# Decay sums of a state space branch: the mask stationary, the masked decays moving in two rounded parts, two step tiles for four

## What is computed

```python
def segsum_exp(a):                       # a: log decays of one chunk of 128 tokens
    cs = jnp.cumsum(a, axis=-1)
    diff = cs[..., :, None] - cs[..., None, :]
    tri = jnp.asarray(np.tril(np.ones((T, T), dtype=bool)))
    return jnp.where(tri, jnp.exp(jnp.where(tri, diff, 0.0)), 0.0)

    # in ssd_chunked, for each chunk c, group g, head r of the group:
    CB = jnp.einsum('bclgn,bcsgn->bcgls', Cc, Bc)
    Wd = CB[:, :, :, None] * segsum_exp(adt)
    y_diag = jnp.einsum('bcgrls,bcsgrp->bclgrp', Wd, xdt)
```

## Time and profile before

| | |
|---|---|
| median of 3 runs | 2958.23 us |
| time of the profiled execution | 2958.16 us |
| its span, first to last instruction | 2956.3 us |
| mean granted TensorE clock | 0.902 of full speed |
| busy share TensorE, VectorE, ScalarE, GpSimd | 82%, 51%, 35%, 12% |
| L1198, the sums: matmul records, busy time | 512, 64.6 us |
| L1525, the steps: instructions, busy time | 64, 67.7 us |

### The profile page before, as it was taken

One profiled execution on the slowest core, in us unless ns is written; L12 is line 12 of the kernel. 1 busy time (PEld: TensorE's weight loads), 2 busy tenths in 40 slices (PEclk: granted clock), 3 DMA queues, 4 the chain that ended last, 5 costly groups with the idle time before them and its releaser, 6 DMA issues. The chain is left out here.

```text
span 2956.3 us, 34644 instructions
## 1 busy us (share of the span) xinstructions
PE 2415.2 (82%) x12559; PEld 1986.6 (67%) x12559; DVE 1515.1 (51%) x2487; ACT 1033.8 (35%) x1661; POOL 343.1 (12%) x474
## 2 busy tenths in 40 slices
PE   6988885888888878585999995997976996856995
PEld 4755564788877867474778773896655986644773
DVE  4254444565566644345233335265875665445664
ACT  3355431333343322143333223263332222214553
POOL 1000000233332200000000000004013431011001
PEclk9998887899999989898999997998988998988997
DMA  4210103111111051212232213213050002237995
GB/s 159 86 47 11 57 1 101 44 57 43 43 43 43 0 213 43 71 58 71 86 99 85 89 53 125 90 43 119 30 174 1 1 1 100 100 122 307 414 419 203
DMA packets 180369, 284.60 MB, mean 96 GB/s; under 512 B 9417, under 2 KB 154649, under 8 KB 170265
## 3 DMA queue, kind: packets, MB, share of 16 engines
q1 hardware_dynamic: 177945, 274.62, 26.7%
q0 software_dynamic: 2304, 8.39, 0.8%
HBM read 240.00 MB, written 42.99 MB: 96 GB/s over the span
## 5 line engine op out<-in xcount | busy, mean ns | idle before, releaser
L146 PE MATMUL ps<-pair,pair 128*128 128x512 f32 (+1 forms) x2504 | 967.6, 386 | 181.4 <-DVE pair L363 73.0
L147 PE MATMUL ps<-pair,pair 128*128 128x512 f32 (+1 forms) x2504 | 932.7, 372 | 0.0
L148 PE MATMUL ps<-pair,pair 128*128 128x512 f32 (+1 forms) x2504 | 931.6, 372 | 0.0
L146 PEld LDWEIGHTS ps<-pair,pair 128*128 128x128 f32 x2504 | 492.2, 197 | 278.3 <-issue 128.1
L147 PEld LDWEIGHTS ps<-pair,pair 128*128 128x128 f32 x2504 | 492.6, 197 | 78.9 <-issue 6.9
L148 PEld LDWEIGHTS ps<-pair,pair 128*128 128x128 f32 x2504 | 490.4, 196 | 80.8
L322 DVE TENSOR_TENSOR pair<-ring,pair 128x2048 fp32r<-128x2048 f32 x104 | 239.8, 2310 | 276.4 <-ACT pair L316 276.3
L316 ACT ACTIVATE pair<-ring 128x2048 fp32r<-128x2048 f32 x104 | 198.0, 1909 | 404.6 <-PE ps L148 341.1
L1532 POOL TENSOR_TENSOR arena<-arena 128x256 f32<-128x256 f32 x64 | 38.8, 640 | 828.3 <-ACT arena L1324 828.3
L721 DVE TENSOR_TENSOR arena<-ps,arena 128x512 f32<-128x512 f32 x56 | 38.7, 692 | 183.1 <-PE ps L148 183.1
L1421 DVE SCALAR_TENSOR_TENSOR arena<-arena 128x512 f32<-128x512 f32 x128 | 96.2, 752 | 21.2 <-issue 20.0
(11 more groups left out here) (431 smaller groups left out, 3498.3 us busy)
## 6 DMA issues: line engine op xcount, KB each, us to landing
ring<-in_w_in SPq DMA_DIRECT2D x54, 1024.0 KB, 6.0
arena<-in_w_exp_down SPq DMA_DIRECT2D x23, 1024.0 KB, 10.9
ring<-in_w_up SPq DMA_DIRECT2D x18, 1024.0 KB, 5.4
ring<-in_w_down SPq DMA_DIRECT2D x16, 1024.0 KB, 5.1
ring<-in_w_exp_gate SPq DMA_DIRECT2D x16, 1024.0 KB, 7.6
ring<-in_w_exp_up SPq DMA_DIRECT2D x16, 1024.0 KB, 9.6
expert_rows<-arena SPq DMA_DIRECT2D x23, 512.0 KB, 6.2
arena<-expert_rows SPq DMA_DIRECT2D x23, 512.0 KB, 10.2
```

The source lines that it names most:

```text
L146: nc.tensor.matmul(out, lhs[1], rhs[0], start=start, stop=False)
L147: nc.tensor.matmul(out, lhs[0], rhs[1], start=False, stop=False)
L148: return nc.tensor.matmul(out, lhs[0], rhs[0], start=False, stop=stop)
```

## The change

The 128x128 mask becomes the stationary operand, and the masked decays of the 4 heads move as one operand of 512 columns. They are held as two fp32r parts (the value rounded, and the rest), so a step takes two matmuls in place of four. The parts of the decays and of the masks GT and LT are made once, before the loop (four small instructions). GpSimd masks both parts, so `steps(n)` is two instructions of 128x512 where it was one. There are two tile pairs for steps in place of four tiles: `steps(n)` waits for `sums(n - 2)`, for n >= 2. GpSimd makes steps 0 and 1 ahead of `xw` 0 and 1, and steps 2 and 3 behind them. In c = 0 of `back`, TensorE and ScalarE now have the feature block first and steps 2 and 3 behind it. The scratch tile `junk` shrinks from four to two parts, with a wait of ScalarE on its own earlier squares.

```diff
@@ -994,6 +994,7 @@
             whole = core.take(2, NT, H)
             bias, alog = core.take(2, H), core.take(2, H)
             dskip = core.take(H)
+            a_parts, strict = core.take_pair(1, 2 * NT * H), core.take_pair(1, P)
             after_dt = core.top
             raw = dt_raw
             u_, a_, b_ = (core.take(NT * 2 * H) for _ in range(3))
@@ -1036,6 +1037,9 @@
                         ins = dve.scalar_tensor_tensor(out=a[:, d, c, :], in0=dt[:, d, c, :], scalar=-1.0,
                                                        in1=alog[:, d, :], op0=ALU.mult, op1=ALU.mult)
                 ins.then_inc(s_a_ready, 1)
+                dve.wait_ge(s_a, 2)
+                dve.tensor_tensor(a_parts.lo[:, 0, :], a.rearrange("p d c h -> p (d c h)"), a_parts.hi[:, 0, :].bitcast(F32),
+                                  ALU.subtract)
                 dve.wait_ge(s_exp, 1)
                 dve.tensor_tensor(wst, wst, dt, ALU.mult)
 
@@ -1043,6 +1047,10 @@
                 act.wait_ge(s_par, 48)
                 act.activation(alog, alog, ACT.Exp).then_inc(s_a, 1)
                 soft_a(act)
+                act.activation(strict.hi[:, 0, :], GT, ACT.Copy)
+                act.activation(strict.lo[:, 0, :], LT, ACT.Copy)
+                act.wait_ge(s_a_ready, 1)
+                act.activation(a_parts.hi[:, 0, :], a.rearrange("p d c h -> p (d c h)"), ACT.Copy).then_inc(s_a, 1)
                 act.wait_ge(s_sums, 1)
                 flat = lambda t: t.rearrange("p d c h -> p (d c h)")
                 act.activation(flat(into), ps[:, 0, 0:2 * NT * H], ACT.Exp)
@@ -1072,11 +1080,11 @@
             xd = core.take(NT, GW)
             prev = core.take(2, NT, GW)
             cb = core.take(2, NT, P)
-            am = core.take(4, GH, P)
+            am = [core.take_pair(1, GH * P) for _ in range(2)]
             ex = core.take(2, GH * P)
             M = xw[:, 2:4].rearrange("p a c n -> p (a c n)").rearrange("p (a n) -> p a n", a=4)
             off = core.take(2, GW)
-            junk = core.take(NT, GW)
+            junk = core.take(2, GW)
             ss, vv, rr, aa = (core.take(NT) for _ in range(4))
             core.top = mark
 
@@ -1194,10 +1202,10 @@
                     if n == 1:
                         after(pe, y_stored, g * 2)
                     after(pe, ex_ready, g * 8 + (n - 1))
-                    for r in range(GH):
-                        mm = nc.tensor.matmul(ps[:, SUMS[n % 2], r * P:(r + 1) * P], am[:, n % 4, r, :],
-                                              (LE, GE)[n % 2], start=True, stop=True)
-                    mm.then_inc(diff_ready, 1)
+                    mask = (strict.hi, strict.lo)[n % 2][:, 0, :]
+                    nc.tensor.matmul(ps[:, SUMS[n % 2], :], mask, am[n % 2].lo[:, 0, :], start=True, stop=False)
+                    nc.tensor.matmul(ps[:, SUMS[n % 2], :], mask, am[n % 2].hi[:, 0, :], start=False, stop=True)\
+                        .then_inc(diff_ready, 1)
 
                 def turn_y(g):
 
@@ -1249,13 +1257,10 @@
 
                 def back(g, between):
                     for c in range(NT):
-                        if c:
-                            between(c)
+                        between(c)
                         if c + 1 < NT:
                             sums(g, 2 * c + 2)
                             sums(g, 2 * c + 3)
-                        if c == 0:
-                            between(c)
                         t = slice(c * P, (c + 1) * P)
                         if c == 0:
                             pe.wait_ge(prev_ready, g + 1)
@@ -1336,17 +1341,16 @@
 
                 def square(g, c):
                     act.wait_ge(y_done, g * 4 + (c + 1))
-                    act.activation(junk[:, c, :], y[:, c, :], ACT.Square, accum_out=ss[:, c:c + 1]).then_inc(ss_ready, 1)
+                    if c >= 2:
+                        act.wait_ge(ss_ready, g * 4 + (c - 1))
+                    act.activation(junk[:, c % 2, :], y[:, c, :], ACT.Square, accum_out=ss[:, c:c + 1]).then_inc(ss_ready, 1)
 
                 def back(g, between):
                     for c in range(NT):
-                        if c:
-                            between(c)
+                        between(c)
                         if c + 1 < NT:
                             decay(g, 2 * c + 2)
                             decay(g, 2 * c + 3)
-                        if c == 0:
-                            between(c)
                         if c:
                             square(g, c - 1)
                     square(g, NT - 1)
@@ -1520,11 +1524,15 @@
                     def steps(n):
 
                         c, d = n // 2, n % 2
-                        if n >= 4:
-                            gp.wait_ge(diff_ready, g * 8 + (n - 3))
-                        gp.tensor_tensor(am[:, n % 4], (GT, LT)[d].unsqueeze(1).to_broadcast([P, GH, P]),
-                                         a[:, d, c, bass.ds(g * GH, GH)].unsqueeze(2).to_broadcast([P, GH, P]),
-                                         ALU.mult).then_inc(am_ready, 1)
+                        if n >= 2:
+                            gp.wait_ge(diff_ready, g * 8 + (n - 1))
+                        for part, out in ((a_parts.lo, am[n % 2].lo), (a_parts.hi, am[n % 2].hi)):
+                            table = part[:, 0, :].bitcast(F32).rearrange("p (d c h) -> p d c h", d=2, c=NT)
+                            ins = gp.tensor_tensor(out.rearrange("p a (r l) -> p (a r) l", r=GH),
+                                                   (LE, GE)[d].unsqueeze(1).to_broadcast([P, GH, P]),
+                                                   table[:, d, c, bass.ds(g * GH, GH)].unsqueeze(2).to_broadcast([P, GH, P]),
+                                                   ALU.mult)
+                        ins.then_inc(am_ready, 1)
 
                     gp.wait_ge(tok_ready, g * 3 + 2)
                     for n, t in ((2, wst), (3, wst)):
@@ -1533,7 +1541,7 @@
                                                    per_head(t, g, n % 2, c), ALU.mult)
                         ins.then_inc(xw_ready, 1)
 
-                    for n in range(4):
+                    for n in range(2):
                         steps(n)
                     for n, t in ((0, dt), (1, dt)):
                         for c in range(NT):
@@ -1541,6 +1549,8 @@
                                                    per_head(t, g, n % 2, c), ALU.mult)
                         ins.then_inc(xw_ready, 1)
 
+                    for n in range(2, 4):
+                        steps(n)
                     for c in range(NT):
                         ins = gp.tensor_tensor(heads(xd[:, c, :]), heads(xt[:, c, :]),
                                                dskip[:, bass.ds(g * GH, GH)].unsqueeze(2).to_broadcast([P, GH, 64]),
```

## The result

The changed kernel takes 3004.35 us (median of 4 runs, 3003.05 to 3006.85) where the kernel before takes 2957.99 us (4 runs, 2956.93 to 2958.32). The ratio is 1.0158, with a 95% interval of 1.0141 to 1.0176: slower by 46 us. The prediction was 3013 us in a range of 2966 to 3032. The profiled execution took 3006.85 us; its span is 3005.1 us, 48.8 more than before.

What follows compares the result with a forecast made beforehand. TensorE bounds `back` and the front half as far as `sums(0)`; VectorE sets the 7.61 us behind. +7.6 us an ordinary iteration, +54.5 in all on 2958.16 gave 3013 us; range 2966 to 3032, the forecast's own 2985 to 3025.

Steps and rivals of the forecast that it cites:

- new sums 4 to 7: Four steps on TensorE's path each save 0.43 us with two fp32r matmuls: -1.7 us an iteration.
- moved sums 2 and 3: Placed behind the feature block, they leave the shadow of VectorE's stretch for TensorE's path: +0.9 us an iteration.
- clock in block 0: TensorE's longer idle gap ahead of the first feature block drops its clock to 0.50: +2.4 us an iteration.
- front half, GpSimd beside the states: GpSimd's doubled steps alternate with VectorE's states and low weights, delaying the first feature matmul: +1.8 us, bounds 0 and 2.4.
- waits in the back half: GpSimd's steps 4 to 7 delay VectorE's mixers, convolution and low weights, so TensorE waits: +4.2 us, lower bound 0.
- clock in block 3: A clock drop inside `back` counted nothing in the sum; a rival priced it at 1.4 us, seven times.
- the second rival: Chance 0.17: rounding costs GpSimd time, or the clock falls inside `back` too; 3022 to 3035 us.
- The last group: With nothing between the steps, GpSimd and VectorE instructions alternate, about 30 us where the window had 24.66: +6 us.
- The first rival: Chance 0.17: GpSimd's work is absorbed, only the clock and moved sums cost; 2965 to 2968 us.
- more than that: Chance 0.17, the second rival: rounding costs GpSimd time (+9 us) or the clock falls inside `back` too (+10 us).
- That L1421 waits: VectorE's convolution instructions in `back` wait for GpSimd: 0.9 us each for the third and fourth; called the weakest ground.
- strict alternation: VectorE and GpSimd instructions take turns, each waiting for the other's; in the last group they sum to 24 us.

Runs made afterwards that it cites:

- number 3: The changed kernel with GpSimd masking only the rounded part in each step, which both matmuls then read; 2969.87 us, ratio 1.0044.
- number 5: The changed kernel with four tile pairs, the old order in c = 0, and GpSimd making steps 0 to 3 ahead of `xw` 0 and 1; 3040.69 us.
- number 1: The changed kernel with TensorE and ScalarE taking steps 2 and 3 ahead of feature block 0 again, as before the change; 2969.87 us, ratio 1.0040.
- number 10: Number 9 with 14 matmuls of 512 columns that nobody reads, filling TensorE's idle time in the gap ahead of block 0; 2954.29 us.
- number 4: The kernel before with the mask stationary alone: one full fp32 matmul of 512 columns a step, no parts, old order; 2965.34 us, ratio 1.0027.
- number 12: Number 7 with 20 matmuls that nobody reads ahead of TensorE's wait on the SiLU; 2932.91 us, ratio 0.9914.
- number 8: Number 5 with GpSimd waiting ahead of `xd` for the exponential of step 1, a short pause; 2970.88 us, ratio 1.0046.
- 6: Number 5 with GpSimd waiting ahead of `xd` until the first mixer of the group is done; 2962.43 us, ratio 1.0015.
- 9: Kernel 6 with steps 0 and 1 ahead of everything else and steps 2 and 3 between `xw` 2, 3 and `xw` 0, 1; 2958.94 us.
- 11: Number 10 with 20 more matmuls that nobody reads ahead of the wait on the SiLU; 2949.21 us, ratio 0.9959.
- 7: The kernel before with GpSimd waiting ahead of `xd` until the first mixer of the group is done; 2945.00 us, ratio 0.9955.

## Why the prediction was right, and where it was off

The mechanisms were the ones named, and 3004 lies in the forecast's own range; that it lies so near to 3013 is in part luck, as the table shows. By its own steps, in an ordinary iteration:

| step | predicted | measured |
|---|---|---|
| new sums 4 to 7 | -1.7 | -1.7 (0.93 for two, 1.78 before) |
| moved sums 2 and 3 | +0.9 | +0.9 |
| clock in block 0 | +2.4 | +1.9 (7.53 - 5.59) |
| front half, GpSimd beside the states | +1.8 | +1.6 (9.17 - 7.61) |
| waits in the back half | +4.2 | +2.6 (1.06 + 1.55) |
| clock in block 3 | 0 | +1.7 (7.16 - 5.46) |
| sum | +7.6 | +6.8 (75.1 - 68.3) |

The waits cost more than their idle time of 0.87 and 1.36 us: from the first L1277 of a block to the L146 behind it are 1.70 us without a wait (930.90 to 932.60), but 2.76 (939.95 to 942.71) and 3.25 (950.09 to 953.34) with one. The terms measured make 7.0, and the front half before `sums(0)` is 0.2 shorter (19.88 for 20.04). The forecast's +4.2 is itself 0.2 too high by its own numbers: VectorE comes at 25.3 where TensorE is ready at 24.4, which is 0.9 and not 1.1 (and the slack of 1.5 us is 12.2 - 10.5 = 1.7, as its 3.2 has it). The upper end of the second rival, 3035, is more than its two terms give (3013 + 10 + 9 = 3032). The first two iterations took 5.1 each more (4.4 and 6.1 predicted). The last group, from `sums(0)` to the work behind its last block, went from 30.52 (1018.17 to 1048.69) to 33.35 us: +2.8, not +6. To the end of its last block, as the forecast counts, it took 27.0 where about 30 was forecast. Seven iterations and the last group make 5.1 + 5.15 + 33.9 + 2.8 = 47 of the span's 48.8; 0.7 is a later first `sums(0)`. The first rival (clock and moved sums alone) falls by the waits; "more than that" was right in one of its parts, the clock inside `back`, and wrong in the other, the cost of rounding.

**That L1421 waits** was the weakest step, and it holds: the fourth takes 1162 ns. But the size was wrong. I charged 0.9 us for each of two, as if each arrived when a GpSimd instruction had just begun. GpSimd started at 938.97, when the third had already been running since 938.48, and the fourth came at 939.52, halfway through: it lost 0.41, about what was left of that instruction. In number 3 one such instruction took 1629 ns, so the 0.9 was a possible size and the meeting was the error. With the mixers at +1.3 in place of +1.7, features 2 came 1.1 and not 3.2 us late. The next pair of mixers lost 1.7 (2.97 us) and not 0.8, so that features 3 came 1.55 late and not 1.1.

The Trainium skill ("SBUF — State Buffer", section "Who interferes with whom") has VectorE instructions with two SBUF inputs contend with GpSimd ones that read SBUF, for a port pair that is an exclusive lock; the second to issue is blocked for the whole of the other instruction. The 1162 ns agree with it in kind; number 5, where one instruction stood through a run of many, goes past what it says.

**The clock in block 3** was left out of the sum. I had counted the clock falling after gaps of 4.6 us and more, and priced it in a rival only for a gap of 3.2. Here it fell behind waits of 0.87 and 1.36 us right behind a block of small matmuls each (25 records with 3.68 us busy in the 5 us before), and in number 1 behind idle times none of which exceeds 2.6. What decides whether it falls, these runs do not settle: in number 10 features 2 took 7.2 us in three iterations and 5.6 in others behind the same wait of 1.07 us, block 0 of number 4 was slow behind the idle times that it was fast behind in the kernel before, and in the kernel before itself the second iteration's took 7.18 us where the later ones, with the same idle times, took 5.59. What they show is that filling idle time brings the clock back: block 0 went from 8.31 to 5.57 us in number 10, the front half from 19.0 or 20.0 to 18.17 in number 12.

**The two errors cancel** (1.6 too much for the waits, 1.7 too little for the clock). That is luck, and the sum looks better than its terms are. The last group's +6 was the other error in the total. It was a sum over strict alternation, and which of its terms was too large was not measured.

**What holds up the gain** is more than the forecast knew. Taken alone, the new form needs GpSimd's work doubled, and this work must lie somewhere. Beside VectorE it makes stalls (after, 5, 8), moved away from it the time saved becomes idle time and a lower clock (6, 9), and with block 0 at full clock it becomes a wait on VectorE or ScalarE (10, 11). What these runs found to gain in the kernel before lay in GpSimd's timing (7) and in the clock (12), not in the sums.

## What to carry to other kernels

Before giving one of GpSimd and VectorE more work, lay their timelines side by side: two-input instructions of the two delay each other, and the long delays came only where GpSimd ran on without a pause while VectorE was on the critical path. A wait that lets GpSimd start once VectorE's urgent stretch is over can be worth more than any saving of work. And a faster TensorE stage inside a gap that another engine ends only lengthens the idle time; read the clock of the block behind the gap before counting the gain.

## What the hardware showed that was not expected

- One VectorE instruction (128x256, two inputs from SBUF, 0.42 us alone) took up to 12.36 us while GpSimd ran without a pause (number 5), and 12.47 in the first iteration of number 8. In other places the two alternated (L1449 at 1.13 us in the changed kernel). In numbers 4 and 8 both kinds of behaviour occurred in one kernel, in number 8 both within unbroken runs. What decides between them stays open: no run changed only the moment at which the two met.
- The clock fell to 1.2 GHz behind idle times of only 0.87 and 1.36 us in one back half, and behind 2.07, 1.44 and 2.44 us in number 1. Behind one wait of 1.07 us in number 10 it was low in three iterations and full in others.
- Matmuls whose results nobody reads made a kernel faster: 2945.00 to 2932.91 us (number 12 against 7) with 20 of them an iteration in front of a wait.
- A GpSimd product of 128x512 rounded to fp32r took 1032 ns at its shortest, 1033 with an fp32 output.
